# Sums over positions of a filter's tap sizes: by VectorE into a running tile, or by TensorE into one PSUM bank

## The reference, cut to what matters

```
h = sin(fr * (z @ w1 + b1)) ... three such layers ...
h = h @ w4                                  # (L, 2 * 512)
h = h * concatenate([decay, decay], axis=-1)
hf, hb = h[:, :512], h[:, 512:]
k = concatenate([hf, zeros((1, 512)), hb[:0:-1]], axis=0)
return k / sum(abs(k), axis=0, keepdims=True)
```

## Time and profile before

| | |
|---|---|
| Median of 3 runs | 1697.88 us (1697.74 to 1698.83) |
| The profiled execution | 1699.96 us |
| Its span, first to last instruction | 1698.1 us |
| Mean granted TensorE clock | 0.965 |
| Busy in the span | TensorE 1582.2 us (93%), VectorE 1032.6 (61%), ScalarE 477.8 (28%), GpSimd 467.6 (28%) |
| Phase of the change | 0 to about 90 us |

### The profile page before, as it was taken

The page is one execution under the profiler, slowest core; times in us unless marked ns, Lnnn a source line. Parts: engine busy times, 40 slices in busy tenths (PEclk is TensorE's granted clock), DMA queues, the critical chain, the costliest instruction groups (busy, mean ns, idle before and its releaser), DMA issues.

```text
span 1698.1 us, 23001 instructions
## 1 busy us (share of the span) xinstructions
PE 1582.2 (93%) x9651; PEld 1465.3 (86%) x9651; DVE 1032.6 (61%) x1394; ACT 477.8 (28%) x666; POOL 467.6 (28%) x198
## 2 busy tenths in 40 slices
PE   4697999999989969899979999999999999999996
PEld 1396889988889969799869999999999999999996
DVE  5868124488833426811678846872885588288846
ACT  1543122222234237541523202211221122022202
POOL 1516111332212139324223313222322213223210
PEclk8788999999989989999989999999999999999999
DMA  8463413342353787520011011011011011101002
GB/s 332 182 258 117 163 58 104 141 155 103 124 179 119 238 241 252 173 96 0 26 50 50 25 50 50 26 50 50 25 50 50 25 50 50 50 26 50 27 36 112
DMA packets 114842, 168.25 MB, mean 99 GB/s; under 512 B 9867, under 2 KB 92067, under 8 KB 109619
## 3 DMA queue, kind: packets, MB, share of 16 engines
q1 hardware_dynamic: 113311, 164.38, 28.6%
q10 hardware_dynamic: 1428, 2.40, 0.4%
HBM read 135.42 MB, written 31.35 MB: 98 GB/s over the span
## 4 chain that ended last, share of the span: by engine, by line
PE 48%; DVE 2%; ACT 1%; POOL 0%; issue 0%; DVEq 0%
PE psum L228 16%; PE psum L232 16%; PE psum L230 16%; DVE mlp_acc_a L2972 1%; POOL ffn_h_lo L2865 0%; PE psum L3168 0%; DVE w_raw L3026 0%; DVE w_raw L3074 0%; ACT w_raw L2918 0%; DVE ffn_h_lo L3036 0%; ACT ffn_h_hi L2922 0%; DVE mlp_acc_a L3026 0%; DVE mlp_acc_a L3074 0%; DVE tail_x L2996 0%; PE psum L3118 0%
## 5 line engine op out<-in xcount | busy, mean ns | idle before, releaser
L228 PE MATMUL psum<-ffn_h_hi,w_hi 128*128 128x320 f32 (+2 forms) x1104 | 267.4, 341 | 12.7 <-DVE mlp_acc_a L2972 11.4
L2972 DVE SCALAR_TENSOR_TENSOR w_raw<-psum,par,w_raw 128x945 f32<-128x945 f32 (+2 forms) x176 | 214.7, 1220 | 93.4 <-ACT w_raw L2893 89.7
L232 PE MATMUL psum<-ffn_h_hi,w_lo 128*128 128x320 f32 (+2 forms) x1104 | 265.6, 339 | 0.0
L230 PE MATMUL psum<-ffn_h_lo,w_hi 128*128 128x320 f32 (+2 forms) x1104 | 265.5, 339 | 0.0
L2972 DVE SCALAR_TENSOR_TENSOR mlp_acc_a<-psum,par,mlp_acc_a 128x945 f32<-128x945 f32 (+2 forms) x176 | 214.5, 1219 | 37.2 <-ACT mlp_acc_a L2893 34.1
L2811 POOL TENSOR_TENSOR w_lo<-w_raw,w_hi 128x2048 fp32r<-128x2048 f32 x32 | 147.9, 4622 | 288.2 <-ACT w_hi L2805 288.2
L228 PEld LDWEIGHTS psum<-ffn_h_hi,w_hi 128*128 128x128 f32 x1104 | 181.6, 189 | 30.6 <-issue 11.6
L230 PEld LDWEIGHTS psum<-ffn_h_lo,w_hi 128*128 128x128 f32 x1104 | 181.4, 189 | 16.5
L232 PEld LDWEIGHTS psum<-ffn_h_hi,w_lo 128*128 128x128 f32 x1104 | 181.2, 188 | 16.4
L2996 DVE SCALAR_TENSOR_TENSOR tail_x<-psum,mod,tail_x 128x384 f32<-128x384 f32 (+1 forms) x192 | 94.8, 515 | 128.3 <-PE psum L232 128.0
L230 PE MATMUL psum<-mlp_g_lo,w_hi 128*128 128x384 f32 x480 | 161.3, 336 | 0.0
(11 more groups left out here) (370 smaller groups left out, 2735.8 us busy)
## 6 DMA issues: line engine op xcount, KB each, us to landing
w_raw<-ffn_w_up SPq DMA_DIRECT2D x22, 1024.0 KB, 5.1
filt_ada<-ada_w SPq DMA_DIRECT2D x16, 1024.0 KB, 8.6
w_raw<-w_in SPq DMA_DIRECT2D x14, 1024.0 KB, 5.5
w_raw<-ffn_w_down SPq DMA_DIRECT2D x11, 1024.0 KB, 5.0
scan_rows_spread<-scratch_scan_rows SPq DMA_DIRECT2D x18, 512.0 KB, 6.0
rownorm_ada<-ada_w SPq DMA_DIRECT2D x8, 1024.0 KB, 6.4
rownorm_x<-x_sample SPq DMA_DIRECT2D x8, 512.0 KB, 8.6
scratch_kt<-kt_spec SPq DMA_DIRECT2D x4, 1024.0 KB, 4.1
```

Source lines behind the costliest of these rows:

```text
L228: ins = nc.tensor.matmul(out, wh, x_hi(k, i), start=begin, stop=False)
L230: ins = nc.tensor.matmul(out, wh, x_lo(k, i), start=False, stop=False)
L232: ins = nc.tensor.matmul(out, wl, x_hi(k, i), start=False, stop=end)
L2972: ins = stt(out=out, in0=image(up_at)[:, r0 + dy:r1 + dy, c0 + dx:c1 + dx], scalar=weight(i, loc, t), in1=out, op0=ALU.mult, op1=ALU.add)
```

## The change

VectorE no longer adds. For every tile, `larger_sizes` writes the larger of the two sizes into one of two halves of `largest`. On TensorE `sum_sizes(j)` multiplies the four pieces of 128 channels of that half by a column of ones and accumulates into columns of bank 5: columns 0 to 3 over tiles 0 to 7, columns 4 to 7 for tile 8. Its place in TensorE's order is two tiles behind: `sum_sizes(j - 2)` follows tile j's product, transposes and parts. The last two groups follow the loop. The eight products at the end, `absum` and the semaphore `norm_mm` are gone; the copy of the sums reads bank 5. The transposes of both modulation groups use bank 4, with a wait for the first group's having been read. ScalarE waits for the larger size of tile j - 2, not for its addition, before it overwrites `size`.

```
--- before.py
+++ after.py
@@ -1464,11 +1464,10 @@
         h_lo = ph.sb("h_lo", [P, FW], F32R)
         w4_hi, w4_lo = k_hi[:, :, NT - 1, :], k_lo[:, :, NT - 1, :]
         summed = ph.sb("summed", [P, 2, 2, DH])
-        largest = ph.sb("largest", [P, DH])
+        largest = ph.sb("largest", [P, 2, DH])
         decay = ph.sb("decay", [P, 2, DH])
         size = ph.sb("size", [P, 2, 2, DH])
         arg, turns = (size[:].rearrange("p a b c -> p (a b c)")[:, i * FW:(i + 1) * FW] for i in range(2))
-        absum = ph.sb("absum", [P, 2, DH])
         norm = ph.sb("norm", [P, 2 * CH])
         zeroed = ph.sem("zeroed")
         wide_zero = ph.sem("layer_w_zeroed")
@@ -1502,15 +1501,14 @@
         k_hi_done = ph.sem("k_hi_done")
         k_lo_done = ph.sem("k_lo_done")
         sized = ph.sem("sizes_done")
+        larger = ph.sem("larger_size_done")
         accumulated = ph.sem("sizes_accumulated")
-        norm_mm = ph.sem("norm_product")
         step_sem = ph.sem("dve_step")
         ps, par = mem["psum"], mem["par"]
         ADA_BANK = 6
         mod = mem["mod"]
 
-        def mod_bank(g):
-            return 5 if g == 1 else 4
+        MOD_BANK, SIZE_BANK = 4, 5
 
         row_place = {1: (4, 0), 0: (5, 0), 2: (5, 1), 3: (5, 2), 4: (5, 3), 5: (4, 1)}
 
@@ -1619,10 +1617,10 @@
                 pe.wait_ge(group_copied, SIDES * (g + 1))
                 if g == 0:
                     pe.wait_ge(par_c, 4)
-                if g >= 2:
-                    pe.wait_ge(mod_done, g - 1)
+                if g:
+                    pe.wait_ge(mod_done, g)
                 for b in range(4):
-                    last = nc.tensor.transpose(ps[:, mod_bank(g), b * P:(b + 1) * P], part_rows[:, g % 2, b * P:(b + 1) * P],
+                    last = nc.tensor.transpose(ps[:, MOD_BANK, b * P:(b + 1) * P], part_rows[:, g % 2, b * P:(b + 1) * P],
                                                mem["ident"][:])
                 last.then_inc(mod_turned, 1)
 
@@ -1636,6 +1634,17 @@
                         last = nc.tensor.matmul(ps[32 * side:32 * side + 2, ADA_BANK + g % 2, :], cond[:, k, :],
                                                 ada[:, p % RING, side * AW:(side + 1) * AW], start=(k == 0), stop=(k == KD - 1))
                     last.then_inc(part_done, 1)
+
+            def sum_sizes(j):
+
+                pe.wait_ge(larger, j + 1)
+                if j == 0:
+                    pe.wait_ge(par_c, 4)
+                for c in range(CH):
+                    at_ = CH * (j // 8) + c
+                    last = nc.tensor.matmul(ps[:, SIZE_BANK, at_:at_ + 1], largest[:, j % 2, c * P:(c + 1) * P], mem["ones"][:, 0:1],
+                                            start=(j == c == 0), stop=(j == NT - 1 and c == CH - 1))
+                last.then_inc(accumulated, 1)
 
             pe.wait_ge(ident_in, 16)
             pe.wait_ge(rows1_in, 16 * n_rows1)
@@ -1666,12 +1675,10 @@
                     turn_group(TURN_AT.index(j))
                 if j >= 1:
                     ada_parts(2 + j)
-            pe.wait_ge(accumulated, NT)
-            for j in range(2):
-                for c in range(CH):
-                    last = nc.tensor.matmul(ps[:, 0, CH * j + c:CH * j + c + 1], absum[:, j, c * P:(c + 1) * P],
-                                            mem["ones"][:, 0:1], start=True, stop=True)
-            last.then_inc(norm_mm, 1)
+                if j >= 2:
+                    sum_sizes(j - 2)
+            sum_sizes(NT - 2)
+            sum_sizes(NT - 1)
 
         @blk.scalar
         def _(act):
@@ -1713,7 +1720,7 @@
                 act.wait_ge(edge, 2 * (1 + j // 8))
                 nc.scalar.activation(k_hi[:, :, j, :], summed[:, j % 2], ACT.Copy).then_inc(k_hi_done, 1)
                 if j >= 2:
-                    act.wait_ge(accumulated, j - 1)
+                    act.wait_ge(larger, j - 1)
                 nc.scalar.activation(size[:, j % 2], summed[:, j % 2], ACT.Abs).then_inc(sized, 1)
                 if j + 2 < NT:
                     act.dma_start(decay[:, j % 2, :], io["k_decay"][j + 2]).then_inc(decay_in[j % 2], 16)
@@ -1753,22 +1760,18 @@
             dve.wait_ge(h_split, 1)
             tt(h_lo[:], h[:], h_hi[:].bitcast(F32), ALU.subtract).then_inc(h_split, 1)
 
-            def accumulate(j):
-
-                first, second = size[:, j % 2, 0, :], size[:, j % 2, 1, :]
+            def larger_sizes(j):
+
                 dve.wait_ge(sized, j + 1)
-                if j in (0, 8):
-                    tt(absum[:, j // 8], first, second, ALU.max).then_inc(accumulated, 1)
-                else:
-                    step.do(tt(largest[:], first, second, ALU.max))
-                    dve.wait_ge(accumulated, j)
-                    tt(absum[:, 0], absum[:, 0], largest[:], ALU.add).then_inc(accumulated, 1)
+                if j >= 2:
+                    dve.wait_ge(accumulated, j - 1)
+                tt(largest[:, j % 2], size[:, j % 2, 0, :], size[:, j % 2, 1, :], ALU.max).then_inc(larger, 1)
 
             def modulation(g):
                 dve.wait_ge(mod_turned, g + 1)
                 at_ = slice(16 * g, 16 * g + 16)
                 out = mod[:, at_, :].rearrange("p (s b) j -> p s b j", s=SIDES)
-                src = ps[:, mod_bank(g), :].rearrange("p (b s j) -> p s b j", s=SIDES, j=32)[:, :, :, 0:2]
+                src = ps[:, MOD_BANK, :].rearrange("p (b s j) -> p s b j", s=SIDES, j=32)[:, :, :, 0:2]
                 bias = par[:, PA["ada_b"]:PA["ada_b"] + BLOCKS][:, at_].rearrange("p (s b) -> p s b", s=SIDES)
                 for j in range(2):
                     ins = tt(out[:, :, :, j], src[:, :, :, j], bias, ALU.add)
@@ -1795,11 +1798,11 @@
                     nc.vector.tensor_copy(second, first).then_inc(edge, 1)
                     dve.wait_ge(edge, 2 * (j // 8) + 2)
                 if j:
-                    accumulate(j - 1)
-            accumulate(NT - 1)
+                    larger_sizes(j - 1)
+            larger_sizes(NT - 1)
             split_forward_lo(nc.vector, 1, slice(UNIT // 2, UNIT))
-            dve.wait_ge(norm_mm, 1)
-            step.do(nc.vector.tensor_copy(norm[:], ps[:, 0, 0:2 * CH]))
+            dve.wait_ge(accumulated, NT)
+            step.do(nc.vector.tensor_copy(norm[:], ps[:, SIZE_BANK, 0:2 * CH]))
             step.do(nc.vector.reciprocal(mem["filter_gain"][:], norm[:]))
             dve.wait_ge(mod_done, PARTS // KD)
             for j in range(2):
```

17 lines of the change are left out of this document (8 added, 9 removed).

## The result

The changed kernel takes 1702.46 us in the median of 19 executions (1699.60 to 1713.92); the kernel before, between them, 1698.19 (1696.38 to 1701.93). The ratio is 1.0037, with an interval of 1.0024 to 1.0051: slower by 6.3 us (4.1 to 8.7), where 1.4 us faster was forecast. The medians lie 4.3 us apart; the ratio also weighs the six executions of the 19 that took more than 1706 us. This spread is new. Over all executions of the changed kernel told of here 20 of 52 took more than 1706 us, while of the kernel before none took more than 1704.85.

A forecast was written before the change was run, and what follows sets the result against it. TensorE was taken to bound the kernel, VectorE mostly this stage, whose gain passes on whole. 1.1 us at the edge plus 0.35 at the end made 1.4 us faster, 1696.5 us; range 1693.4 to 1699.8.

The forecast's parts named there:

- The bound of the stage and who sets the loop: Stage from 40 to 90 us: TensorE takes over the loop from VectorE; the kernel gains or loses what the stage does.
- The removed adds: VectorE's loop: seven adds go, 11.0 us at most; ninth tile's taps 2.5 us earlier, 1.0 to 1.1 us kept.
- The price of a group: Four products with ones on TensorE, per tile: 0.9 us at the high clock, 1.79 at the low.
- Rival C: TensorE's loop: a group costs 1.79 us at the high clock too; 1.5 us slower, 1699.4 us; chance 0.17.
- the clock still rising: TensorE's loop: first group from 53.1 us takes 1.3 us as the clock rises; full clock then expected until 75 us.
- Rival D: TensorE's clock falls: low from 67 us on gives 1702 us, low in the whole loop 1713; chance 0.08.
- The edge beside GpSimd: Edge steps after the last taps: second waits for GpSimd until 79.1 us, edge done at 79.9; 1.0 to 1.1 us kept.
- The last wait: Stage's end: the copy of the sums no longer waits for TensorE's products with ones, 0.38 us less.

The follow-up runs named there:

- the control: The kernel before run again without edit, against itself, with a second trace: 1699.07 us, ratio 0.9997.
- streamed, no tail: Changed kernel with each group one product streaming 512 sizes against ones, final copy and turning of sum rows left out (sums wrong): 1697.07 us.
- b: Changed kernel, no edit, one of four executions profiled singly: 1699.02 us.
- fourth: One of the traces of the changed kernel, no edit: 1706.31 us.
- c: Changed kernel, no edit, one of four executions profiled singly: 1709.68 us.
- adds kept: Changed kernel with VectorE's seven additions made as before, result unused: 1706.13 us, then 1703.56 in a second run.

## Why the prediction was wrong, step by step

**The bound of the stage and who sets the loop: right.** TensorE took over from VectorE, each pair of taps from tile 3 on waited for it, and the stage's length was handed on: against the control the profile after is 3.4 us later at the copy of the sums and 3.8 at the end of the span.

**The removed adds: right in kind.** 2.1 us at the end of the stage without the groups, 2.1 to 3.5 us with all of them moved; forecast were 1.4 us with them in place. With groups in place and the clock high throughout (streamed, no tail) it was 0.7, since the taps came at 76.62 and not at 75.5.

**The price of a group: right.** 0.98 us at the high clock against 0.9, 1.80 at the low against 1.79. Rival C, a group of 1.79 us at the high clock, is refuted. Tile 8's product was to end at 75.4; where the clock stayed high (streamed, no tail) it ended at 76.6 with groups of 1.05 us, and the taps followed at once.

**The failed step: "the clock still rising" at 53.1 and full until 75.** I took the rise at 53.5 us of the one trace of before as given, and let the groups inherit it. With groups the clock rose at 61 to 62 in nine of ten traces of such kernels apart from the doubled one. It fell again in the middle of full work in all ten, near 75 us in six of them. Even in b, whose rise at 53.7 us was the assumed one and whose first group took the forecast 1.3 us, it fell at 70.7, as tile 7's product began. In the profile after, this accounts for the late ninth tile. Until 61.15 the group, tile 3's product and two parts took 8.2 us (52.95 to 61.15) in place of the forecast 1.3 + 1.74 + 1.83 = 4.9: 3.3 us. From 75.4 on the rest of tile 7's product, the transposes, a group and tile 8's product took until 81.8, 6.4 us, where 0.5 + 0.55 + 0.9 + 1.74 = 3.7 would do at the high clock: 2.7 us. Together 6.0 of the 6.4 us between 75.5 and 81.88.

**Rival D came nearest, with 0.08.** Its cause, the clock, was right. That its price agrees (4 us later at the ninth tile; 3.8 measured) is luck: D let the clock fall at 67 us after an early rise, or stay low through the whole loop, while in the profile after it rose 8 us late and fell at 75.4. No rival had a late rise, and it made 3.3 of the 6.0 us. What misled me was that the loop has no pause. The clock fell without one. D had the mechanism of the spread too, up to 1713 us, but the range ended at 1699.8 and left D out.

**The edge beside GpSimd: right where it could be seen.** In the profile after the taps came after GpSimd's work, and the second edge step took its 0.42 us. In the kernel with the groups moved it was issued at 76.13 and took 1.37 us, to 0.27 us behind GpSimd's end at 77.23: with one input in SBUF it waited like the adds. In "streamed, no tail" it took 1.37 us too. Forecast was an edge of 4.4 us from the start of the taps (75.5 to 79.9); it took 4.0 (73.93 to 77.95), where it takes 2.9 undisturbed. The Trainium skill ("SBUF — State Buffer", SBUF: two separate sides) gives the shared ports as an exclusive lock, under which one of the two blocks until the other is done; these numbers agree with it.

**The last wait: right.** The copy of the sums waited 0.38 us for TensorE before and does not now.

**Left open.** Whether the clock rises at 54 or at 61 us goes in part with what it did before the groups, as the first column of the table shows, and without such groups nothing else is seen (53.5 to 54.5 against 57.8 to 58.5). Why b rose at 53.7 and the fourth, c and "adds kept" at 61, with 0.50 in that column in all four, stays open.

The totals keep 0.5 to 1.4 us of the 2.1 to 3.5 that the moved groups win in the stage. Part of this is decided behind the stage. From the copy of the sums to the end of the span it is 1606.0 to 1611.8 us in the eighteen traces, 1609.3 and 1606.0 in the two of before. VectorE's pair of instructions at line 1213 behind one of 3.57 us at line 571 starts at 163.73 us in the first of these and at 161.73 in the second, although the stage had ended 0.1 us apart. TensorE's clock was low until 146 us in the one and until 140 in the other (the first trace, then the second):

```profile
140.00:150.00 10.00, 9.17 (x50) 7.82 (x48) 8.69 (x11) 4.72 (x9) 7.34 (x9) 0.71 0.46 74
140.00:150.00 10.00, 8.84 (x60) 7.33 (x59) 9.86 (x15) 6.07 (x11) 9.30 (x10) 0.98 0.35 34
```

The first kernel with the groups moved is 3.4 us ahead of the control at the copy and 1.4 at that pair (160.36), with the clock low until 142 us. That the clock makes these differences is argued from the traces; no run was made for it. So how much of the executions between 1706 and 1716 us comes from the stage is known for single traces only: c lost 9.2 us there of some 10, but "fourth" took 1706.31 with 3.9 lost in the stage.

## What to carry to other kernels

Before work is put into a loop on TensorE, ask not only how long it occupies the engine but what clock it leaves. Four products of one column and one product of 512 columns occupied it for the same microsecond here; with the first the stage ended 1 to 10 us later than with the second, mostly 4, as the clock went. A single trace's clock is one draw: where the forecast needs the clock to be high, price the low clock as a case of its own, above all when the change uses up the slack that made the kernel indifferent to it. And put such work into the engine's pauses, if memory allows: with the same groups there the stage ended as early as without them (85.28 and 86.60 us against 86.66).

## What the runs showed of the hardware that was not expected

TensorE's granted clock was 1.2 GHz for long stretches with the engine busy in every hundredth of them: it averaged 0.53 from 75 to 83 us in the profile after, 0.63 from 61 to 75 us in c, 0.50 there with the groups doubled, and it fell at 70.7 us in b. With one product of 512 columns in place of each group and the same full busy time it was 1.00 from 61 to 75 us. The Trainium skill ("TensorE: Matmul & The Clock Gate", What's actually happening) says that the gate follows how busy TensorE has been, and that its phase against the kernel varies. The traces agree with the variation (rises at 53.5 and at 58.5 us in the same kernel before). With the first they agree only if busy means something else than the profile's busy time.
